# Second layer's experts: down products 512 columns wide over two neighbouring weight slots, and the transposes of a group of h one piece later

## What is computed

```python
g, idx = lax.top_k(jnp.swapaxes(aff, 1, 2), cap)
...
xe = hf[flat].reshape(b, N_EXPERTS, cap, d)
a = jnp.einsum('becd,edf->becf', xe, w_gate)
u = jnp.einsum('becd,edf->becf', xe, w_up)
y = jnp.einsum('becf,efd->becd', jax.nn.silu(a) * u, w_down)
y = y * g[..., None].astype(y.dtype)
out = jnp.zeros((b * n, d), y.dtype).at[flat].add(y.reshape(-1, d))
```

## Time and profile before

| | |
|---|---|
| median of 3 runs | 3531.35 us |
| lowest, highest | 3527.01, 3535.99 us |
| profiled execution | 3528.74 us |
| its span | 3527.0 us |
| TensorE busy | 3017.9 us, 86% |
| VectorE busy | 2070.8 us, 59% |
| ScalarE busy | 1789.4 us, 51% |
| mean granted TensorE clock | 0.925 of full speed |

### The profile page before, as it was taken

The page is one execution under the profiler, slowest core; times in us unless marked ns, Lnnn a source line. Parts: engine busy times, 40 slices in busy tenths (PEclk is TensorE's granted clock), DMA queues, the critical chain, the costliest instruction groups (busy, mean ns, idle before and its releaser), DMA issues. The chain is left out here.

```text
span 3527.0 us, 59842 instructions
## 1 busy us (share of the span) xinstructions
PE 3017.9 (86%) x24750; PEld 2464.0 (70%) x24750; DVE 2070.8 (59%) x2213; ACT 1789.4 (51%) x2016; POOL 514.9 (15%) x250
## 2 busy tenths in 40 slices
PE   6599787986999999999999759983948999999993
PEld 2488653542888888888887647661528999999993
DVE  0422375334666766666666454553355888888884
ACT  2411154232555555555555356673236677777773
POOL 1011133002011112111211113331020000000000
PEclk8699899987999999999999869996968999999997
DMA  7211100228787878787777521002246999999995
GB/s 322 73 36 36 54 1 26 90 91 341 252 273 265 274 266 268 261 272 269 261 262 261 168 84 36 30 18 72 91 172 233 369 359 355 365 380 357 356 357 178
DMA packets 137950, 726.07 MB, mean 206 GB/s; under 512 B 10708, under 2 KB 13524, under 8 KB 109828
## 3 DMA queue, kind: packets, MB, share of 16 engines
q1 hardware_dynamic: 125064, 684.99, 52.0%
q0 software_dynamic: 12288, 37.75, 4.5%
q10 hardware_dynamic: 384, 0.24, 0.0%
HBM read 680.90 MB, written 42.04 MB: 205 GB/s over the span
## 5 line engine op out<-in xcount | busy, mean ns | idle before, releaser
L1539 DVE TENSOR_TENSOR mixed_low<-mixed_raw,mixed_high 128x3072 fp32r<-128x3072 f32 (+1 forms) x192 | 593.3, 3092 | 352.2 <-ACT mixed_high L1473 349.4
L1473 ACT CAST mixed_high<-mixed_raw 128x3072 fp32r<-128x3072 f32 (+1 forms) x192 | 489.9, 2554 | 483.2 <-DMA mixed_raw<-in_moe 482.9
L1960 DVE TENSOR_TENSOR rows_low<-rows_raw,rows_high 128x2816 fp32r<-128x2816 f32 x188 | 581.3, 3093 | 80.0 <-ACT rows_high L1904 70.4
L1904 ACT CAST rows_high<-rows_raw 128x2816 fp32r<-128x2816 f32 x188 | 479.3, 2559 | 112.6 <-PE ps L1811 64.2
L1395 PE MATMUL ps<-mixed_high,mixed_xhi 128*128 128x384 f32 (+1 forms) x1024 | 343.3, 335 | 0.5 <-DVE mixed_low L1539 0.5
L1809 PE MATMUL ps<-rows_high,rows_xhi 128*128 128x352 f32 x1024 | 337.4, 329 | 6.0 <-issue 4.5
L1811 PE MATMUL ps<-rows_high,rows_xlo 128*128 128x352 f32 x1024 | 330.0, 322 | 0.0
L1397 PE MATMUL ps<-mixed_high,mixed_xlo 128*128 128x384 f32 (+1 forms) x1024 | 329.6, 322 | 0.0
L1810 PE MATMUL ps<-rows_low,rows_xhi 128*128 128x352 f32 x1024 | 329.6, 322 | 0.0
L1396 PE MATMUL ps<-mixed_low,mixed_xhi 128*128 128x384 f32 (+1 forms) x1024 | 329.6, 322 | 0.0
L1383 PE MATMUL ps<-mixed_raw,mixed_xc 128*32 128x96 f32 (+1 forms) x8192 | 188.0, 243 | 42.4 <-ACT mask_sb L1495 28.2
(11 more groups left out here) (286 smaller groups left out, 5895.2 us busy)
## 6 DMA issues: line engine op xcount, KB each, us to landing
rows_raw<-in_moe_rows SPq DMA_DIRECT2D x192, 1408.0 KB, 7.9
mixed_raw<-in_moe SPq DMA_DIRECT2D x144, 1536.0 KB, 6.4
ring_r<-in_ada_w SPq DMA_DIRECT2D x24, 2048.0 KB, 17.4
mixed_raw<-in_moe SPq DMA_DIRECT2D x48, 1024.0 KB, 6.5
w_raw_r<-in_ev_in SPq DMA_DIRECT2D x18, 512.0 KB, 3.2
w_raw_u<-in_od_in SPq DMA_DIRECT2D x16, 512.0 KB, 3.3
x_res<-ring_r SPq DMA_DIRECT2D x10, 512.0 KB, 2.6
x_norm<-ring_r SPq DMA_DIRECT2D x10, 512.0 KB, 2.9
```

The source lines that it names most:

```text
L1473: act.copy(r.high[:, p % SLOTS, 0:nj, :], r.raw[:, p % SLOTS, 0:nj, :]).then_inc(high_done, 1)
L1539: dve.tensor_tensor(r.low[:, p % SLOTS, 0:nj, :], r.raw[:, p % SLOTS, 0:nj, :], r.high[:, p % SLOTS, 0:nj, :].bitcast(F32), ALU.subtract). ...
L1904: act.copy(high[:, p % SLOTS, :], raw[:, p % SLOTS, :]).then_inc(high_done, 1)
L1960: dve.tensor_tensor(low[:, p % SLOTS, :], raw[:, p % SLOTS, :], high[:, p % SLOTS, :].bitcast(F32), ALU.subtract).then_inc(low_done, 1)
```

## The change

It does three things.
1. `down` takes two pieces at once: it waits for both, multiplies the 11 blocks of hT with 512 columns that lie in two neighbouring slots, into one PSUM bank, and marks both pieces done at the end. It is called for p = 2 and p = 4 instead of for 2, 3, 4, 5.
2. With that, `turn_x` stands behind the second of these calls, thus behind all four down pieces.
3. The transposes of group u-1 stand behind the up piece of unit u, not between its gate and its up piece. Lines of the changed kernel are one or so off those of the kernel before. The copies and splits of the groups are moved on ScalarE and VectorE: groups 0 and 1 to places 8 and 10, group 2 to place 0 of the next turn, group 3 to place 1 of it.

```diff
--- before.py
+++ after.py
@@ -1826,20 +1826,19 @@
 
             def down(e, p):
 
-                q = p - DOWN[0]
-                if q == 0:
+                half = (p - DOWN[0]) // 2
+                if half == 0:
                     pe.wait_ge(hT_high, e * UNITS)
                     pe.wait_ge(hT_low, e * UNITS)
-                if q % 2 == 0:
-                    pe.wait_ge(y_read, e * 2 + (q // 2 - 1))
-                ready(e, p)
-                wh = high[:, p % SLOTS, :].rearrange("p (j n) -> p j n", j=FJ)
-                wl = low[:, p % SLOTS, :].rearrange("p (j n) -> p j n", j=FJ)
-                n = D // 4
+                pe.wait_ge(y_read, e * 2 + (half - 1))
+                ready(e, p + 1)
+                s = p % SLOTS
+                wh = high[:, s:s + 2, :].rearrange("p s (j n) -> p s j n", j=FJ)
+                wl = low[:, s:s + 2, :].rearrange("p s (j n) -> p s j n", j=FJ)
+                out = m.ps[:, 4 + half, :].rearrange("p (s n) -> p s n", s=2)
                 for j in range(FJ):
-                    mm = products(m.ps[:, 4 + q // 2, (q % 2) * n:(q % 2 + 1) * n], hT_hi[:, j, :], hT_lo[:, j, :],
-                                  wh[:, j, :], wl[:, j, :], j == 0, j == FJ - 1)
-                mm.then_inc(piece_done, 1)
+                    mm = products(out, hT_hi[:, j, :], hT_lo[:, j, :], wh[:, :, j, :], wl[:, :, j, :], j == 0, j == FJ - 1)
+                mm.then_inc(piece_done, 2)
 
             def turn_h(e, g):
 
@@ -1872,15 +1871,15 @@
                     turn_h(e - 1, 3)
                 if expert(e):
                     up(e, b, 1, 0, 1)
-                for p in DOWN:
+                for p in (2, 4):
                     if later(e):
                         down(e, p)
                     if p == 4 and (not isinstance(e, int) or e + 1 < NE):
                         turn_x(e + 1)
                 for u in range(1, UNITS) if expert(e) else ():
                     up(e, b, 4 + 2 * u, u, 0)
+                    up(e, b, 5 + 2 * u, u, 1)
                     turn_h(e, u - 1)
-                    up(e, b, 5 + 2 * u, u, 1)
 
             turn_x(0)
             turns(pe, turn)
@@ -1931,13 +1930,15 @@
 
             def turn(e, b):
                 for p in range(TURN):
+                    if p == 0 and later(e):
+                        copy_h(e - 1, 2)
+                    if p in (8, 10) and expert(e):
+                        copy_h(e, p // 2 - 4)
                     if p == 0 or p in (6, 8, 10):
                         if expert(e):
                             silu(e, p, max(0, p // 2 - 2))
-                    if p == 0 and later(e):
+                    if p == 1 and later(e):
                         copy_h(e - 1, 3)
-                    if p in (6, 8, 10) and expert(e):
-                        copy_h(e, p // 2 - 3)
                     if p == 4 and (not isinstance(e, int) or e + 1 < NE):
                         copy_x(e + 1, 1 - b)
                     q = p + SLOTS
@@ -1995,12 +1996,14 @@
 
             def turn(e, b):
                 for p in range(TURN):
+                    if p == 0 and later(e):
+                        split_h(e - 1, 2)
+                    if p in (8, 10) and expert(e):
+                        split_h(e, p // 2 - 4)
                     if p in (1, 7, 9, 11) and expert(e):
                         multiply(e, p, (p - 5) // 2 if p > 1 else 0)
-                    if p == 0 and later(e):
+                    if p == 1 and later(e):
                         split_h(e - 1, 3)
-                    if p in (6, 8, 10) and expert(e):
-                        split_h(e, p // 2 - 3)
                     if p in (3, 5) and later(e):
                         weigh(e - 1, p // 2 - 1)
                     if p == 4 and (not isinstance(e, int) or e + 1 < NE):
```

## The result

The change is slower: a median of 3625.19 us (four runs, 3620.26 to 3638.33) against 3532.22 us (four runs of the kernel before beside it), ratio 1.028 with an interval of 1.026 to 1.030. That is 93 us more. The profiled executions are 3620.26 and 3528.74 us, 91.5 apart; the forecast was +87.

The account below looks back on a forecast made before the run. The prediction took TensorE as the bound, with VectorE nearly full behind it and its instruction order deciding. It added 80 us of longer turns and 7 us of clock to 3528.7 us, giving 3616 us, range 3585 to 3640.

Parts of the forecast that it names:

- What bounds it: Second layer's experts: TensorE busy 784.25 of 819 us, VectorE behind it with hardly any slack; what waits ahead of its instructions decides.
- The wide products: Down products: 1056 of 512 columns at 226.7 ns save 14.1 us; the two-slot operand was taken to cost nothing.
- The coarser release: Transposes of x come behind four down pieces, not three; TensorE then waits some 1.5 us a turn for piece 8.
- The transfers: Next turn's pieces 1 and 3 land +23.7 and +30.9 us after the transposes of x, behind scatter and gather.
- The order on VectorE: Group 3's split stands behind piece 4's low part: down products at +40.9 us, a turn 55.9 us instead of 50.3.
- The wait ahead of group 3: TensorE, ahead of group 3's transposes, waits some 3.2 us a turn for VectorE's product of unit 3.
- The wait ahead of the down products: TensorE, after piece 1, waits some 3.1 us a turn for VectorE's split of group 3.
- The clock: Half-rate stretches after TensorE's new stalls cost 1.7 us in four of fifteen turns, 7 us in all.
- The sum: Second layer's experts: fourteen turns add 78 us, the first about 2 less, the tail about 4 more: 80 us.
- Rival 3: Transfer queue not in the chain: pieces land some 1.5 us earlier, 58 us more than before, about 3588 us; chance 0.08.
- Rival 4: Clock falls at both stalls of every turn, on the path: 51 us over the 80, 3660 us; chance 0.05.
- Rivals 1 and 2: First: split of group 3 ready within piece 1, 3485 us, chance 0.04; second: effects cancel, near 3533 us, chance 0.03.

Follow-up runs that it names:

- e3: The change with copy and split of group 3 ahead of cast and low part of the next turn's piece 4: 3581.91 us, ratio 1.014.
- e4: The kernel before with only the moved transposes, and group 3's copy and split ahead of the next turn's piece 4: 3524.73 us, ratio 0.999.
- e5: e1 with ten plain matmuls filling TensorE's wait ahead of the transposes of group 1: 3570.70 us, ratio 1.012.
- e10: The change with the second half of the output weighed ahead of the low part of piece 8: 3610.87 us, ratio 1.023.
- e11: e4 with the second half of the output weighed ahead of the low part of piece 8: 3501.20 us, ratio 0.993.
- e9: The change with ten plain matmuls ahead of the transposes of group 3 and ten more ahead of the down products: 3616.28 us, ratio 1.025.
- e6: The change with ten plain matmuls ahead of the transposes of group 3: 3639.43 us, ratio 1.032.
- e1: The kernel before with only the 512-column down products in pairs and the transposes of x behind all four pieces: 3596.59 us, ratio 1.019.
- e7: e3 with the transposes of x between the two pairs of down pieces: 3552.56 us, ratio 1.008.
- e2: The kernel before with only the transposes a piece later and the copies and splits moved as in the change: 3595.60 us, ratio 1.018.

## Why the prediction was right

- **What bounds it.** Right: TensorE was no less busy after, and the order of VectorE's list set the time. The two orders were tested apart (e3 and e4 for group 3; e5 for the late transposes of x).
- **The wide products.** They are 228 ns apart (66 in 15.07 us), against 226.7 in the earlier trace rows: the two-slot operand costs about nothing. The Trainium skill (TensorE: Matmul & The Clock Gate, Back-to-back issue gap) gives about 216 ns for an isolated product of 512 columns and about 131 ns in a sustained stream; the rows agree with neither, and they decide.
- **The coarser release.** Right: 1.5 us forecast ahead of piece 8, 1.48 measured; the wait ahead of group 1 gone. e5 shows the longer run alone: 14.99 less 11.88 is 3.1 us a turn, and 3.1 us is its mean turn over that of before.
- **The transfers.** Landings 0.2 and 0.3 us later than forecast. The weighing and the scatter behind it were treated as fixed links; moving them was worth 14 us (e10) and 24 us (e11).
- **The order on VectorE.** Right in kind, a little short in size. The wait ahead of group 3 was 3.2 forecast, 3.16 measured. For the down products I had "low part to between +39.5 and +40.0", with low part 3 followed at once by low part 4. The split of group 2 stands between them (2990.21, 0.46 us to the next start), as the order of instructions had shown. That and the 0.3 us of the landing put the down products at +41.5 and +41.3, not +40.9; the run took 15.07, not 14.97. A turn is 56.4 to 56.6 us, and 56.1 to 56.3 with both waits filled (e9), not 55.9: some 5 us over 15 turns, **the term that was mis-sized**. The wait ahead of the down products was 1.86 us, not 3.1, because piece 1 ran at half rate and ended later; with piece 1 at full rate it is 3.27 (e6).
- **The clock.** The 7 us were about right, some 6 by e9, but that was luck: the reason was wrong. I took half rate in four turns of fifteen on the path, behind the second wait. It is there in two. In the other twelve it comes behind the first, and piece 1 covers most of it. "After the second it lies on the path" is what e6 shows, at 14 us.
- **The sum.** The 14 turns from the second to the last transposes of x took 87.1 us more (795.0 against 707.9), the tail behind them 4.5 (4 forecast), 91.5 in all. Less the clock's 6 that is 85 us of chain, where 80 were forecast, and so the forecast fell 4.5 us short of the profiled execution. The range was added up wrongly: 3616 with 14 and 18 more is 3648, not 3640; the result lies in both.
- **The rivals.** Rival 3 needed landings 1.5 us earlier: they weren't. Rival 4 needed half rate on the path twice a turn: once, covered. Rivals 1 and 2 needed the split of group 3 to be early. With it early, and narrow products, the moved transposes come out even (e4), so the 29.3 us of waiting that they were to save wasn't to be had from TensorE's order alone.

What stays open: the kernel before with the early weighing alone wasn't tried, so how much of e11's 29 us needs e4's order is not known. Nor is it known how much of e11's gain is the earlier scatter and how much the weighing that VectorE now does in a wait. Nor is it shown whether the pairs lose, beside the clock, by the transfers or by the coarser release itself.

## What to carry to other kernels

Where two engines are both near full, write out the loop as a chain from one fixed event to the same event a turn later, with every instruction that stands in each in-order list, small ones too; a step that is put behind a long one in such a list can cost that one's whole length. Ask of each moved step which wait it could fill and which transfers it starts: moving one weighing of 1.05 us, with its scatter, was worth 24 us in e4's order, more than the 14 us that the wide products could save on TensorE. Judge a wait by where the half-rate stretch behind it falls, and don't add the costs of two parts that share one such stretch.

## What the runs showed of the hardware

- Waits of 3.0 to 3.8 us ahead of a transpose were followed by a stretch at half rate in nearly every turn of the change, e1 and e3, and those of 1.2 to 1.6 us by none in any kernel. In e7 four waits of 3.0 to 3.4 us passed without one (turns from 3027.80 to 3232.52), so the length of the wait alone doesn't decide it. The price of one was 1.5 to 1.7 us where the work behind it was on the path (e1, e2, e6), and some tenths of a microsecond where another engine was waited for anyway (most turns of the change). Filling one wait made the next one longer, and the half rate moved there.
- A plain float32 matmul of 128 columns is two records of some 120 ns each: ten of them are 20 records in 2.39 us. As filling they are cheap to write and occupy TensorE for 0.24 us apiece.
- A 1408 KB transfer asked for at +10.4 was in by +17.0 where the scatter of 128 rows left behind it, at +11.2 (e4), and landed at +18.4 and +19.7 where scatter and gather left ahead of it, at +6.9 and +8.8 (e11, e10).
